# Block inversion of the RWKV recurrence in four 32x32 diagonal blocks per head, heads in one group

## What is computed

```python
def step(s, inp):
    r_t, w_t, k_t, v_t, kk_t, b_t = inp
    sa = jnp.einsum('bhvk,bhk->bhv', s, kk_t)
    s = s * w_t[:, :, None, :] - sa[..., None] * b_t[:, :, None, :] + v_t[..., None] * k_t[:, :, None, :]
    return s, jnp.einsum('bhvk,bhk->bhv', s, r_t)
```

## Time and profile before

| | |
|---|---|
| runs | 2140.99, 2145.52, 2148.98 us; median 2145.52 |
| profiled execution, first to last instruction | 2142.3 us |
| busy: PE, PEld | 1925.8 us (90%), 1415.1 us (66%) |
| busy: DVE, POOL, ACT | 1017.1, 690.1, 494.8 us (47, 32, 23%) |
| recurrence, ten units | about 596 to 1263 us |

### The profile page before, as it was taken

The page is one execution under the profiler, slowest core; times in us unless marked ns, Lnnn a source line. Parts: engine busy times, 40 slices in busy tenths (PEclk is TensorE's granted clock), DMA queues, the critical chain, the costliest instruction groups (busy, mean ns, idle before and its releaser), DMA issues. The chain is left out here.

```text
span 2142.3 us, 40499 instructions
## 1 busy us (share of the span) xinstructions
PE 1925.8 (90%) x15900; PEld 1415.1 (66%) x15900; DVE 1017.1 (47%) x2092; ACT 494.8 (23%) x936; POOL 690.1 (32%) x1036
## 2 busy tenths in 40 slices
PE   7999989897899999999999977998699999999966
PEld 2565655464677777777777756944487888887732
DVE  3868675658345444543455343746612222222228
ACT  2111132030233333433333312101121212121100
POOL 4526000000043323423243222322234454444435
PEclk9999999899899999999999988998899999999988
DMA  8233656473141211122111018620199989998855
GB/s 283 59 129 128 210 177 233 143 274 94 47 141 42 80 47 51 41 67 70 47 47 28 8 43 298 229 98 30 62 370 339 327 300 315 343 345 313 324 218 241
DMA packets 228304, 355.64 MB, mean 166 GB/s; under 512 B 38306, under 2 KB 156853, under 8 KB 224453
## 3 DMA queue, kind: packets, MB, share of 16 engines
q1 hardware_dynamic: 201358, 300.73, 41.1%
q0 software_dynamic: 24496, 45.01, 6.0%
q10 hardware_dynamic: 2310, 7.92, 1.0%
HBM read 307.11 MB, written 84.34 MB: 183 GB/s over the span
## 5 line engine op out<-in xcount | busy, mean ns | idle before, releaser
L2829 DVE TENSOR_TENSOR me_hh<-me_sg,ps_ju 128x128 f32<-128x128 f32 x76 | 21.9, 288 | 388.3 <-PE ps_jd L2781 376.8
L452 PE MATMUL ps_s<-hT,w_in_sb 128*128 128x512 f32 x432 | 196.6, 609 | 0.0
L2773 PE MATMUL ps_jg<-me_xT,me_wg 128*128 128x128 f32 x1216 | 150.8, 278 | 0.0
L2773 PE MATMUL ps_ju<-me_xT,me_wu 128*128 128x128 f32 x1216 | 148.2, 275 | 0.0
L1349 PE MATMUL ps_gs<-hT,gt_w 128*128 128x512 f32 x256 | 143.6, 644 | 3.2 <-PEq L76 3.2
L2781 PE MATMUL ps_jd<-me_wd,me_hh 128*128 128x512 f32 x304 | 143.1, 593 | 2.4 <-DVE me_yb L2835 2.4
L452 PEld LDWEIGHTS ps_s<-hT,w_in_sb 128*128 128x128 f32 x432 | 82.4, 196 | 94.7 <-issue 94.1
L2773 PEld LDWEIGHTS ps_jg<-me_xT,me_wg 128*128 128x128 f32 x1216 | 144.7, 195 | 0.0
L2773 PEld LDWEIGHTS ps_ju<-me_xT,me_wu 128*128 128x128 f32 x1216 | 141.9, 192 | 0.0
L2050 POOL TENSOR_TENSOR rc_lj<-rc_l,rc_lev 128x256 f32<-128x256 f32 x100 | 73.8, 758 | 174.7 <-PE ps_c L1742 174.3
L2802 ACT ACTIVATE me_xT<-ps_jx 128x1024 f32<-128x1024 f32 x77 | 78.9, 1025 | 211.1 <-PE ps_jx L2764 211.1
(11 more groups left out here) (568 smaller groups left out, 3965.2 us busy)
## 6 DMA issues: line engine op xcount, KB each, us to landing
me_wg<-in_exp_w_gate SPq DMA_DIRECT2D x76, 512.0 KB, 5.5
me_wu<-in_exp_w_up SPq DMA_DIRECT2D x76, 512.0 KB, 8.2
me_wd<-in_exp_w_down SPq DMA_DIRECT2D x76, 512.0 KB, 6.1
w_ad_sb<-in_w_ada SPq DMA_DIRECT2D x32, 512.0 KB, 4.0
w_in_sb<-in_w_in SPq DMA_DIRECT2D x31, 512.0 KB, 4.5
gt_w<-in_w_in SPq DMA_DIRECT2D x24, 512.0 KB, 4.4
cb_rows<-yj_dram SPq DMA_DIRECT2D x6, 2048.0 KB, 22.0
zr<-in_w_ada SPq DMA_DIRECT2D x4, 2048.0 KB, 9.3
```

The source lines that it names most:

```text
L452: mm(ps_s[:, b, :], w_in[:, r, k, :], hT[:, k, 0:TS], start=(k == 0), stop=(k == KT - 1))
L2773: last = mm(o[:, 0:P], w[:, s, k, :], xT[:, s % 2, k, :], start=(k == 0), stop=(k == KT - 1))
```

## The change

- Until level 4, `xi` and `yi` hold four 32x32 diagonal blocks per head, one in each quarter of the partitions, for both heads of all pairs: 128 partitions x 256 elements instead of 512. Levels 0 to 3 work on them. The group loop `g` is gone: each product, copy, update, mask and semaphore is one for all heads, and a product has 32 matmuls of 32 x 32 x 32 where it had 16 (both groups) of 64 x 64 x 64.
- Level 4 couples the 32 blocks in pairs to 64 blocks: 16 matmuls for the first and second product (two blocks), 8 for the third (one block). The results and, through six copies by ACT (`expand`), the diagonal blocks go into 64-wide buffers `yx` (now two, by direction), `yc64` and `x64`, which DVE clears once at the start. Level 5 and the solve read these.
- The first Gram product only fills what is read: for each quarter its diagonal block and the one beside it (32 matmuls, 64 columns), then the coupling block (8 matmuls of 64 x 64 x 64). The second only the four diagonal blocks (32 matmuls, 32 columns). The other three are as before.
- `lj` is the second half of the rows of `gg`. The masks `levc` and `idc` are cut in quarters.

The diff, cut; only semaphore counts, the last level's copies of group 1 and the same changes on POOL and ACT are left out.

```diff
-        lo, lc, xi, yi, yx, gg, lj = (sb(x, [P, 2, MT, HD]) for x in
-                                      ("rc_l", "rc_lc", "rc_x", "rc_y", "rc_yx", "rc_g", "rc_lj"))
-        levc, idc = sb("rc_lev", [P, 2, LJ, HD]), sb("rc_id", [P, HD])
+        lo, lc, gg, x64, yc64 = (sb(x, [P, 2, MT, HD]) for x in ("rc_l", "rc_lc", "rc_g", "rc_xh", "rc_yh"))
+        xi, yi = sb("rc_x", [P, 2, MT, SB]), sb("rc_y", [P, 2, MT, SB])
+        g32, lj = gg[:, :, :, 0:SB], gg[:, :, :, SB:HD]
+        yx = sb("rc_yx", [P, 2, 2, MT, HD])
+        levc, idc = sb("rc_lev", [P, 2, LJ - 1, SB]), sb("rc_id", [P, SB])
...
+        def wide(x):
+            return x.unsqueeze(1).unsqueeze(1).to_broadcast([P, 2, MT, SB])
+
...
+        quarter = [slice(c * SB, (c + 1) * SB) for c in range(4)]
+
+        def blocks(d):
+
+            return [(quarter[2 * b + 1 - d], quarter[2 * b + d]) for b in range(2)]
+
+        def within(block):
+
+            return slice(block.start % HD, block.start % HD + SB)
...
-                    for k, (l, r) in enumerate(((a_, b_), (b_, a_), (k_, a_), (k_, r_), (b_, r_))):
-                        if k == 0 and n:
-                            pe.wait_ge(m.c_un, n)
-                            pe.wait_ge(m.c_s, n)
-                        if k == 1 and n:
-                            pe.wait_ge(m.c_y, n * 2)
+                    rows, cols = coupling(d)
+                    if n:
+                        pe.wait_ge(m.c_un, n)
+                        pe.wait_ge(m.c_s, n)
+                    for q in range(MT):
+                        for c, own in enumerate(quarter):
+                            for e in range(2):
+                                both = b_[half[e], q, half[c // 2]].rearrange("p (s i) -> p s i", s=2)
+                                mm(bank[e][own, q, 0:HD].rearrange("p (s i) -> p s i", s=2), a_[half[e], q, own],
+                                   both if c % 2 == 0 else both[:, ::-1], start=True, stop=True)
+                    for q in range(MT):
+                        for e in range(2):
+                            last = mm(bank[e][rows, q, HD:P], a_[half[e], q, rows], b_[half[e], q, cols], start=True, stop=True)
+                            if q == MT - 1:
+                                last.then_inc(m.c_gr, 1)
+                    if n:
+                        pe.wait_ge(m.c_y, n * 2)
+                    for q in range(MT):
+                        for c, own in enumerate(quarter):
+                            for e in range(2):
+                                last = mm(bank[2 + e][own, q, 0:SB], b_[half[e], q, own], a_[half[e], q, own], start=True, stop=True)
+                                if q == MT - 1 and c == 3:
+                                    last.then_inc(m.c_gr, 1)
+                    for k, (l, r) in ((2, (k_, a_)), (3, (k_, r_)), (4, (b_, r_))):
...
+                        if j == LJ - 1:
+                            pe.wait_ge(m.c_exp, n * 3 + 1)
+                        for q in range(MT):
+                            for e in range(2):
                                 if j == LJ - 1:
-                                    last = mm(bank[g][cols, q, 0:HD], lc[rows, g, q, :], yi[rows, g, q, :], start=True, stop=True)
+                                    last = mm(bank[e][cols, q, 0:HD], lc[rows, e, q, :], yx[rows, d, e, q, :], start=True, stop=True)
+                                elif j == LJ - 2:
+                                    for r32, c32 in blocks(d):
+                                        last = mm(bank[e][c32, q, 0:SB], lo[r32, e, q, SB:HD], yi[r32, e, q, :], start=True, stop=True)
                                 else:
-                                    for b in half:
-                                        last = mm(bank[g][b, q, 0:HD], lj[b, g, q, :], yi[b, g, q, :], start=True, stop=True)
-                            last.then_inc(m.c_g, 1)
+                                    for b in quarter:
+                                        last = mm(bank[e][b, q, 0:SB], lj[b, e, q, :], yi[b, e, q, :], start=True, stop=True)
+                        last.then_inc(m.c_g, 1)
...
+                        if j == LJ - 1:
+                            pe.wait_ge(m.c_exp, n * 3 + 3)
+                        for q in range(MT):
+                            for e in range(2):
+                                if j == LJ - 1:
+                                    last = mm(bank[e][cols, q, 0:HD], x64[cols, e, q, :], gg[cols, e, q, :], start=True, stop=True)
+                                elif j == LJ - 2:
+                                    for r32, c32 in blocks(d):
+                                        last = mm(bank[e][c32, q, 0:SB], xi[c32, e, q, :], g32[c32, e, q, :], start=True, stop=True)
                                 else:
...
+                                    for b in quarter:
+                                        last = mm(bank[e][b, q, 0:SB], xi[b, e, q, :], g32[b, e, q, :], start=True, stop=True)
+                        last.then_inc(m.c_yg, 1)
+                        if j < LJ - 1:
                             for q in range(MT):
...
+                                for e in range(2):
+                                    if j == LJ - 2:
+                                        r32, c32 = blocks(d)[cols.start // HD]
+                                        last = mm(bank[2 + e][r32, q, 0:SB], g32[c32, e, q, :], xi[c32, e, q, :], start=True, stop=True)
+                                    else:
+                                        for b in quarter:
+                                            last = mm(bank[2 + e][b, q, 0:SB], g32[b, e, q, :], xi[b, e, q, :], start=True, stop=True)
+                            last.then_inc(m.c_xg, 1)
...
-                    V.tensor_copy(levc[b], m.lev[b, :, 0:LJ, b])
+                for b in quarter:
+                    V.tensor_copy(levc[b], m.lev[b, :, 0:LJ - 1, b])
                     V.tensor_copy(idc[b], m.ident[b, b])
+                V.memset(yx[:], 0.0)
+                V.memset(yc64[:], 0.0)
+                V.memset(x64[:], 0.0)
...
+                    if n:
+                        dve.wait_ge(m.c_exp, n * 3)
+                    mk = wide(levc[:, 1 - d, 0])
+                    V.tensor_tensor(yi[:], banks[:, 2:4, :, 0:SB], mk, ALU.mult).then_inc(m.c_gd, 1)
...
+                        rows, cols = coupling(d)
+                        dve.wait_ge(m.c_yg, n * LJ + j + 1)
+                        if j < LJ - 2:
                             if j == 0:
-                                dve.wait_ge(m.c_y1, n * 2 + g + 1)
-                            if j == LJ - 1:
-                                V.tensor_scalar(yx[cols, g], bank[g][cols, :, 0:HD], -1.0, None, ALU.mult).then_inc(m.c_yup, 1)
-                            else:
-                                V.tensor_tensor(yi[:, g], yi[:, g], bank[g][:, :, 0:HD], ALU.subtract).then_inc(m.c_yup, 1)
-                                dve.wait_ge(m.c_xg, n * (2 * LJ - 2) + 2 * j + g + 1)
-                                V.tensor_tensor(xi[:, g], xi[:, g], bank[2 + g][:, :, 0:HD], ALU.subtract).then_inc(m.c_xup, 1)
+                                dve.wait_ge(m.c_y1, n + 1)
+                            V.tensor_tensor(yi[:], yi[:], banks[:, 0:2, :, 0:SB], ALU.subtract).then_inc(m.c_yup, 1)
+                            dve.wait_ge(m.c_xg, n * (LJ - 1) + j + 1)
+                            V.tensor_tensor(xi[:], xi[:], banks[:, 2:4, :, 0:SB], ALU.subtract).then_inc(m.c_xup, 1)
+                        elif j == LJ - 2:
+                            of_rows, of_cols = blocks(d)[rows.start // HD], blocks(d)[cols.start // HD]
+                            V.tensor_scalar(yx[of_rows[1], d, :, :, within(of_rows[0])], banks[of_rows[1], 0:2, :, 0:SB], -1.0, None,
+                                            ALU.mult)
+                            V.tensor_scalar(yc64[of_cols[1], :, :, within(of_cols[0])], banks[of_cols[1], 0:2, :, 0:SB], -1.0, None,
+                                            ALU.mult).then_inc(m.c_yup, 1)
+                            dve.wait_ge(m.c_xg, n * (LJ - 1) + j + 1)
+                            V.tensor_scalar(x64[of_cols[0], :, :, within(of_cols[1])], banks[of_cols[0], 2:4, :, 0:SB], -1.0, None,
+                                            ALU.mult).then_inc(m.c_xup, 1)
+                        else:
+                            V.tensor_scalar(yx[cols, d], banks[cols, 0:2, :, 0:HD], -1.0, None, ALU.mult).then_inc(m.c_yup, 1)
...
+                def expand(n, rows, cols):
+
+                    d = n % 2
+                    act.wait_ge(m.c_yup, n * LJ + LJ - 2)
+                    for b in blocks(d)[rows.start // HD]:
+                        last = A(yx[b, d, :, :, within(b)], yi[b], ACT.Identity)
+                    last.then_inc(m.c_exp, 1)
+                    for b in blocks(d)[cols.start // HD]:
+                        last = A(yc64[b, :, :, within(b)], yi[b], ACT.Identity)
+                    last.then_inc(m.c_exp, 1)
```

(15 more changed lines are left out.)

102 lines of the change are left out of this document (34 added, 68 removed).

## The result

The changed kernel takes 2232.72 us (median of 4 runs, 2225.02 to 2237.85) against 2147.25 us before: ratio 1.040, 95% interval 1.036 to 1.044. It is 85 us slower where 37 us faster was forecast. The profiled execution spans 2235.3 us. The first view is the head of its page: the span, PE's and PEld's busy time, the granted clock in 40 slices, and the queue that brings instructions (packets, MB).

A forecast was written before the change was run, and what follows sets the result against it. TensorE (PE), busy 627 of 672 us in the recurrence, was taken as the bound. PE's saving of 67 us, less 18 lost to attention and 4, 2 and 6 added, gave -37 us: 2108 us, range 2090 to 2126.

The forecast's parts named there:

- Products of the levels: In levels 0 to 3 a product falls from 0.93 to 0.51 us; levels together save 6.3 us a unit.
- Steps in parallel on many tiles: On TensorE, narrow tiles run steps at once: four tiles in the levels (0.51 us a product), eight in the Gram products.
- the gain of the Gram products: The first Gram products of a unit take 1.6 us instead of 2.0, saving 0.4 us a unit.
- Column price: On TensorE, 0.83 ns per column plus 5 ns fixed: a step of 32 columns takes 32 ns.
- Lost to attention: TensorE time saved in gaps where it waits for attention becomes idle instead: 18 us lost.
- Small terms: Added waits: expanding copies on ACT +4 us, DVE's clears +2 us once, single-group copies left uncovered +6 us.
- Rival 3, the supply: TensorE can't be fed: 29 ns a pass gives +107 us (2250), 19 ns gives +41 us (2186); chance 0.06.
- The clock: Over the ten units the granted clock stays near 0.97; if it falls, steps cost up to double; no chance given.
- B3: Theory from follow-up runs, not the forecast: clock goes with array work (columns times tile area), not PE's busy time.

The follow-up runs named there:

- narrow1: Changed kernel with half as many matmuls in levels 0 to 3, each of 64 columns on 32x32 tiles (results wrong): 2184.53 us.
- wideshort: Kernel before, 64x64 tiles, with only 32 of 64 columns in products, copies and updates of levels 0 to 3 (results wrong): 2196.18 us.
- the burst: Kernel before with 256 matmuls on two 64x64 tiles, then 512 on four 32x32 tiles, ahead of the first unit: 2186.62 us, single run.
- l4wide: level4 with the same 32 columns in level 4's matmuls, but on 64x64 tiles instead of 32x32: 2183.01 us.
- spread: Changed kernel with the attention step between first and second product moved between second and third: 2242.93 us.
- oldgram: Changed kernel with the first two Gram products of the kernel before: 2217.83 us.
- l4fill: level4 with two zero-weight matmuls of 128x128 by 128 columns ahead of most softmax waits: 2180.05 us.
- narrowlong: narrow1 with 128 columns in each matmul of levels 0 to 3, still on 32x32 tiles (results wrong): 2195.73 us.
- k1quad: Kernel before with the second Gram product only in its 64x64 diagonal blocks, on four 64x64 tiles: 2143.00 us, ratio 0.999.
- level4: Kernel before with k1quad's second Gram product and level 4 only on its 32x32 blocks; levels 0 to 3 unchanged: 2180.52 us.
- afterwide: Changed kernel with seven unread matmuls of 128x128 by 256 columns added a unit, in levels 0 to 4: 2206.61 us.
- l4pad: level4 with two unread matmuls of 128x128 by 256 columns a unit added ahead of level 4's second products: 2163.67 us.

## Why the prediction was wrong

- **Products of the levels: right in time.** 64 passes take 0.55 to 0.58 us for 0.51, and the forecast's unit of 63 to 64 us is seen in narrow1 where the clock holds (62.6 us, one unit of nine).
- **Steps in parallel on many tiles: wrong, and it cost the gain of the Gram products.** They took 0.79, 0.61 and 0.69 us, 2.09 in all, for 0.60, 0.60 and 0.40, 1.6 in all. The two that missed are those on eight tiles. Their passes start 10.2 ns (64 columns) and 9.0 ns (32 columns) apart, where eight tiles at 58 and 32 ns a step would give 7.3 and 4. Four 32x32 tiles gave 8.5 to 8.9 ns. So twice the tiles started no faster, and whether the 8.5 ns of the levels are a step of 34 ns on each of four tiles, as forecast, or a pace of PE that happens to lie beside it, no run separates: hitting it may be luck.
- **Column price: wrong as a law.** It was worked out from 512, 128 and 64 columns and carried to 32. On 64x64 tiles the step is 58 ns for 32 columns as for 64 (wideshort). The forecast used 32 columns on narrower tiles alone, so this cost it nothing.
- **Lost to attention: right in size.** 18 us forecast; narrow1 waits 45.0 us at L1499 for 24.5, +20. The changed kernel itself waits 29.5 us; PE's own work lasts longer there at half clock.
- **Small terms.** The expanding copies took 0.41 us each for 0.38, and PE waited 1.0 us in all for level 5's operands. DVE's clears took 1.9 us, but the first Gram product came 0.4 us later, not 2: POOL's inputs weren't late by as much. PE waited 0.5 us for the copies of the single group at level 4. Together they are far under the 12 us put down.
- **Rival 3, the supply: dismissed by a wrong step.** It took 29 ns from the lasting pace of two 64x64 tiles and set it aside because nine passes started 19 ns apart. Those nine rightly show that the array can start faster, but they say nothing of a lasting supply: in the burst 128 passes start 8.5 ns apart, and then PE waits. The text said itself that they "bound the feed from one side only", and still gave 0.06. That the supply too comes to 29 ns a pass (3.73 us for 128) is a coincidence as far as the runs show. Its price is 40 us of pauses, less than the 107 of a feed without store: a unit needs about 11 packets of 3.73 us in 77 us, so the supply is short only where products follow each other closely.
- **The clock: named, not priced.** "The granted clock over the ten units should stay near 0.97" got no reason, and "every step costs up to double, and the forecast is wrong whatever the overlap" stood under what would show it, with no chance and no sum. That is the failing step: a term put at nothing. The clock came to 0.81, 266 us more at half. wideshort gives the price, since its products last as long as before: 129 us more at half clock made its recurrence 47 us longer (720 for 673), 0.36 us for each (its copies and updates are shorter too, so that may be low). As an estimate that is 97 us here; with the pauses of 40 us 137. The recurrence grew by 94, so -43 are left, near the -37 of the forecast. What the forecast put at nothing, clock and supply, is the whole miss; the Gram gain that wasn't there and small terms under their 12 us nearly cancel.
- As busy as before isn't enough: wideshort and l4wide leave PE idle for 38 and 47 us, the kernel before for 45, and lose the clock.

What stays open: B3 orders most of the kernels. From 7.05 and 7.00 (clock 0.953 and 0.950) over 6.88, 6.66 and 6.51 (0.943, 0.930, 0.924) to 5.87 and 5.81 (0.915, 0.899), the clock falls with the work. The changed kernel, spread and oldgram, with 21 to 40 us of pauses, lie lowest (0.899 to 0.908). l4fill (6.93, 0.934) lies below that row and narrowlong (6.08, 0.927) above it, so where the work stands, and what the area of a tile counts, isn't settled. How a fall once begun lasts 3 us at one place and 37 at another (wideshort, 1025 us) wasn't either. No run beat the kernel before beyond its interval; k1quad is equal to it.

## What to carry to other kernels

A count of busy microseconds was not enough here: ask also what the array works per microsecond (columns times tile area) after the change, above all next to stretches that are thin already, and give a fall of the clock a price and a chance. A kernel at 0.98 can be near the edge: here level4 was to save 17 us of PE's time and cost 34 us. And a matmul cut into smaller ones costs supply: count instructions per stretch, and compare bursts with the lasting rate, not with the fastest few starts in a trace.

## What the hardware showed that I had not expected

- PE's instructions arrive in batches of 256 every 3.73 us, at times 4.0, when it waits for them (burst).
- Passes start 8.5 ns apart on four 32x32 tiles and no closer on eight 64x32 tiles (9.0 ns), 29 ns on two 64x64 tiles, and the latter the same for 32 and 64 columns. The Trainium skill ("TensorEngine Tiling (Array Packing)", Instruction Overhead) puts the cost of small matmuls at some 60 cycles each, 25 ns at 2.4 GHz as an estimate. Taken for one tile the trace doesn't contradict it (34 ns from pass to pass on one of four); taken for PE as a whole it does.
- Twice, adding work that nobody reads made the kernel faster: afterwide by 26 us, l4pad by 17.
- Leaving out half the columns of levels 0 to 3, on the same tiles and with as many matmuls (wideshort), made the kernel 49 us slower.
